# A hybrid decoder layer on one core: a reordered preparation, a fused second norm and an output projection cut into pieces

## The reference: what is computed

```
h     = rms_norm(x, norm1_g) * (1 + scale1) + shift1
x_lru, g_lru, q_lat, kv_lat, k_rope = split(h @ w_in)
lru   = rg_lru(causal_dwconv(x_lru)) * gelu(g_lru)          # recurrent half, 512 columns
attn  = latent attention(q_lat, kv_lat, k_rope, cache)      # attention half, 8 heads
mixed = concat(rms_norm(lru), rms_norm(attn)) @ w_o
x     = x + gate1 * mixed
h2    = rms_norm(x, norm2_g) * (1 + scale2) + shift2
up    = causal_dwconv(h2 @ w_up);  val, gt = split(up)
x     = x + gate2 * ((gelu(gt) * val) @ w_down)
```

## Time and profile before

| what | us |
|---|---|
| median of 3 runs | 986.07 |
| the runs | 986.3, 986.07, 982.07 |
| the profiled execution, its own time | 985.16 |
| its span, first to last instruction | 983.4 |
| busy in it: PE / DVE / ACT / POOL | 945.4 / 656.3 / 526.5 / 192.8 |

### The profile page before, as it was taken

One profiled execution on the slowest core, in us unless ns is written; L12 is line 12 of the kernel. 1 busy time (PEld: TensorE's weight loads), 2 busy tenths in 40 slices (PEclk: granted clock), 3 DMA queues, 4 the chain that ended last, 5 costly groups with the idle time before them and its releaser, 6 DMA issues.

```text
span 983.4 us, 20621 instructions
## 1 busy us (share of the span) xinstructions
PE 945.4 (96%) x7984; PEld 881.0 (90%) x7984; DVE 656.3 (67%) x1253; ACT 526.5 (54%) x1183; POOL 192.8 (20%) x192
## 2 busy tenths in 40 slices
PE   4799999899999999999999999999999999999997
PEld 2488876699999999999898989999999999999997
DVE  2695278478988988989873576777777777722221
ACT  2332854399889898898873333444444443312110
POOL 0022222133334333433340230010001001000000
PEclk9799999899999999999999989999999999999999
DMA  9968642400202202122121432333333332652202
GB/s 326 340 200 253 199 155 82 156 1 23 87 23 108 87 23 88 54 77 87 44 65 45 108 58 66 104 87 85 85 85 85 95 106 59 165 146 60 63 3 87
DMA packets 106289, 100.13 MB, mean 102 GB/s; under 512 B 7119, under 2 KB 94943, under 8 KB 104126
## 3 DMA queue, kind: packets, MB, share of 16 engines
q1 hardware_dynamic: 102422, 77.91, 27.2%
q0 software_dynamic: 3456, 20.97, 6.0%
q10 hardware_dynamic: 340, 0.27, 0.1%
HBM read 96.41 MB, written 2.94 MB: 101 GB/s over the span
## 4 chain that ended last, share of the span: by engine, by line
PE 88%; DVE 5%; ACT 3%; DMA 2%; issue 1%; SPq 0%; POOL 0%; DVEq 0%; ACTq 0%
PE ps L909 51%; PE ps L1297 19%; PE ps L904 7%; PE ps L942 2%; PE ps L1204 2%; PE ps L1255 2%; DMA RW<-w_ada 2%; PE ps L1292 1%; PE ps L1079 1%; PE ps L1230 1%; PE ps L915 1%; DVE normed_low L1904 1%; DVE RB L1878 0%; ACT RB L1493 0%; DVE RB L2334 0%
## 5 line engine op out<-in xcount | busy, mean ns | idle before, releaser
L909 PE MATMUL ps<-normed_high,up_weights_high 128*128 128x260 f32 x704 | 142.3, 283 | 0.2
L909 PE MATMUL ps<-normed_high,up_weights_low 128*128 128x260 f32 x704 | 142.0, 283 | 0.0
L909 PE MATMUL ps<-normed_low,up_weights_high 128*128 128x260 f32 x704 | 141.8, 283 | 0.0
L849 POOL TENSOR_TENSOR latents_low<-RB,latents_high 128x512 fp32r<-128x512 f32 (+1 forms) x72 | 86.2, 1197 | 163.9 <-ACT latents_high L1628 159.7
L1744 ACT ACTIVATE up_weights_high<-RW 128x1024 fp32r<-128x1024 f32 x44 | 46.5, 1060 | 133.5 <-PE ps L909 133.5
L1297 PE MATMUL ps<-key_weights_high,latents_high 128*128 128x260 f32 x528 | 116.4, 302 | 0.8 <-ACT RB L1675 0.7
L909 PEld LDWEIGHTS ps<-normed_high,up_weights_high 128*128 128x128 f32 x704 | 108.6, 189 | 0.8 <-DVE normed_low L1904 0.6
L909 PEld LDWEIGHTS ps<-normed_high,up_weights_low 128*128 128x128 f32 x704 | 108.6, 189 | 0.0
L909 PEld LDWEIGHTS ps<-normed_low,up_weights_high 128*128 128x128 f32 x704 | 108.3, 188 | 0.0
L1297 PE MATMUL ps<-key_weights_low,latents_high 128*128 128x260 f32 x528 | 106.4, 283 | 0.0
L1297 PE MATMUL ps<-key_weights_high,latents_low 128*128 128x260 f32 x528 | 106.4, 283 | 0.0
(11 more groups left out here) (331 smaller groups left out, 2197.1 us busy)
## 6 DMA issues: line engine op xcount, KB each, us to landing
RW<-w_ada SPq DMA_DIRECT2D x24, 1024.0 KB, 7.2
RW<-w_up SPq DMA_DIRECT2D x44, 512.0 KB, 5.0
RW<-w_down SPq DMA_DIRECT2D x8, 1408.0 KB, 7.2
RW<-w_in SPq DMA_DIRECT2D x11, 512.0 KB, 8.2
RB<-w_o SPq DMA_DIRECT2D x8, 512.0 KB, 4.1
RB<-x_prompt SPq DMA_DIRECT2D x2, 1024.0 KB, 13.3
o_y_p<-RB SPq DMA_DIRECT2D x4, 512.0 KB
cst<-consts SPq DMA_DIRECT2D x1, 845.0 KB, 11.6
```

The lines of the kernel that those rows point to most:

```text
L849: nc.gpsimd.tensor_tensor(latL[:, g % 3, c:4 * P], turned[:, g % 3, c:4 * P], latH[:, g % 3, c:4 * P].bitcast(F32), ALU.subtract).then_inc ...
L909: last = mm(ps[j % 4][rows[0]:rows[1], h, 0:H], lhsT, src[:, h * H:(h + 1) * H], start=start, stop=stop)
```

## The change

It edits three places.

**The preparation.** PE's order becomes: keys and values 0, the last modulation columns, keys and values 1, qst, keys and values 2, qa, keys and values 3, spread, three fillers, stored rows 0 to 3 with a filler behind each, the norm sum nlru, and only then the last stored rows. The copies of the stored rows go from VectorE to ScalarE. The squares of the recurrent half are added by GpSimd into one tile (three additions), and nlru is two matmuls in place of eight. GpSimd takes the samples' new rows later, inside unit 0. The slots of the jobs are dealt anew.

**The last softmax.** `recurrent_half` becomes `recurrent_part(m, ks)`, which runs only some of the four tiles. The eight fillers between the softmax's links give way to pieces of output tiles 1 and 2.

**The second norm.** VectorE makes x times gain times root in one instruction for all eight tiles; ScalarE adds the shift and writes the high part at once; VectorE makes the low part from the unrounded product, shift and high part. GpSimd's four products are gone. On PE the eight fillers ahead of the up-projection are gone, the first round of the loop is written out, and its first two jobs go through the tiles k as they become ready, the second job four tiles behind the first.

```diff
-PREP_ORDER = [("c5", 1), ("qst", 3), ("l0", 1), ("l1", 3), ("l2", 1), ("l3", 3), ("kv2", 2), ("kv3", 0), ("qa", 1), ("spread", 3),
-              ("l4", 1), ("l5", 3), ("l6", 2), ("nlru", 0)]
+PREP_ORDER = [("c5", 3), ("qst", 3), ("kv2", 1), ("qa", 3), ("kv3", 2), ("spread", 0), ("l0", 3), ("l1", 0), ("l2", 3), ("l3", 0),
+              ("nlru", 1), ("l4", 3), ("l5", 0), ("l6", 3)]
-J_NMLA, J_VP = job(2), job(3)
-J_WO = [job(n) for n in (0, 1, 7, 6, 4, 5, 11, 10)]
-J_N2, J_FST = job(KT), job(KT + 1)
+J_VP, J_NMLA = job(3), job(7)
+J_WO = [job(n) for n in (0, 1, 2, 11, 4, 5, 6, 8)]
+J_N2, J_FST = job(9), job(10)
...
@@ gpsimd @@
-            pool.wait_ge(s_clr, 4)
-            pool.wait_ge(s_new, 16)
+            for k in range(1, LT):
+                pool.wait_ge(s_sq, KT + 4 + k + 1)
+                if k > 1:
+                    pool.wait_ge(s_lrn, k - 1)
+                nc.gpsimd.tensor_tensor(lru_sq[:, 0, :], lru_sq[:, 0, :], lru_sq[:, k, :], ALU.add).then_inc(s_lrn, 1)
...
+                    if u == 0 and g == 1:
+                        pool.wait_ge(s_clr, 4)
+                        pool.wait_ge(s_new, 16)
+                        for n in range(2):
+                            new_key(n, n)
+                            new_latent(n, n)
...
-            pool.wait_ge(s_rs, 7)
-            for k in range(KT // 2, KT):
-                nc.gpsimd.tensor_tensor(h2[:, k, 0:NP], xT[:, k, 0:NP], rs[:, 0:NP], ALU.mult).then_inc(s_hq, 1)
@@ tensor @@
             keys_and_values(2)
-            keys_and_values(3)
...
+            keys_and_values(3)
             claim(pe, J_SPREAD)
...
+            keep_busy(spare, 3)
+            pe.wait_ge(s_kr, 2)
+            for a in range(4):
+                stored_rows(a)
+                keep_busy(spare, 1)
+            claim(pe, J_NLRU)
+            pe.wait_ge(s_lrn, LT - 1)
+            both(J_NLRU, ones, lru_sq[:, 0, :], True, True).then_inc(psum_full[J_NLRU % 4], 1)
             stored_rows(4)
...
-            for m in range(2):
-                pe.wait_ge(key_free[m], KEY_JOBS // 3)
-                recurrent_half(m)
-            pe.wait_ge(key_free[2], KEY_JOBS // 3)
+            recurrent_part(0, range(LT))
+            recurrent_part(1, (0,))
             turn_max(NS)
-            keep_busy(ps[2][:, 0, 0:2 * P], 2)
+            recurrent_part(1, (1,))
             spread_max(NS)
-            keep_busy(ps[2][:, 0, 0:2 * P], 4)
+            recurrent_part(1, (2, 3))
             pv(NS)
-            keep_busy(ps[2][:, 0, 0:2 * P], 2)
+            recurrent_part(2, (0,))
...
+            recurrent_part(2, (1,))
             pe.wait_ge(s_ol, 1)
...
-            recurrent_half(2)
+            recurrent_part(2, (2, 3))
             norm_sum(J_NMLA, LT, KT + 8)
-            recurrent_half(3)
+            recurrent_part(3, range(LT))
...
-            claim(pe, up_job(0), 0)
-            keep_busy(flat(up_job(0))[:, 0:2 * P], 8)
...
+            for k in range(KT):
+                pe.wait_ge(s_hlo, KT + k + 1)
+                up_products(0, 0, k)
+                if k >= KT // 2:
+                    up_products(0, 1, k - KT // 2)
+            for k in range(KT // 2, KT):
+                up_products(0, 1, k)
...
+            with pe.Fori(1, FT // 2) as i:
@@ scalar @@
+            def stored_rows(a):
...
+                A(otok[0:n, a, :], flat(j)[0:n, 0:KV + ROPE], ACT.Copy).then_inc(psum_free[j % 4], 1)
...
+            stored_rows(0)
             prep_rstd(8, HEADS)
+            for a in range(1, 4):
+                stored_rows(a)
             rstd(J_NLRU, LW).then_inc(s_rs, 1)
+            stored_rows(4)
+            stored_columns(0, 9)
+            stored_columns(1, 11)
...
-                A(h2[:, k, 0:NP], h2[:, k, 0:NP], ACT.Identity, bias=modT[:, 3 * KT + k, 0:1], scale=gmod[:, k, 0:1]).then_inc(s_h, 1)
+                act.wait_ge(s_hp, KT + k + 1)
+                A(hH[:, k, 0:NP], h2[:, k, 0:NP], ACT.Identity, bias=modT[:, 3 * KT + k, 0:1]).then_inc(s_h, 1)
@@ vector @@
+            def scaled(k):
+                V.scalar_tensor_tensor(h2[:, k, 0:NP], xT[:, k, 0:NP], gmod[:, k, 0:1], rs[:, 0:NP], MUL, MUL).then_inc(s_hp, 1)
+            def normed_low(k):
+                dve.wait_ge(s_h, KT + k + 1)
+                V.scalar_tensor_tensor(hL[:, k, 0:NP], h2[:, k, 0:NP], modT[:, 3 * KT + k, 0:1], hH[:, k, 0:NP].bitcast(F32), ADD, SUB).then_inc(s_hlo, 1)
...
+            for k in range(KT):
+                normed_low(k)
+                if k + 2 < KT:
+                    scaled(k + 2)
```

More of the change, by code:

```diff
@@ L836, in new_latent @@
                 nc.gpsimd.tensor_copy(lat[e][0:1, PAGES, :], newrow[0:1, s, 0:KV]).then_inc(s_newc, 1)
-            for n in range(2):
-                new_key(n, n)
-                new_latent(n, n)
             def low_latents(u, g):
@@ L1158, in _ @@
             stored_columns(1, XX, NP, 11)
-            j = J_NLRU
-            claim(pe, j)
-            for k in range(LT):
-                pe.wait_ge(s_sq, KT + 4 + k + 1)
-                last = both(j, ones, lru_sq[:, k, :], k == 0, k == LT - 1)
-            last.then_inc(psum_full[j % 4], 1)
             def kclaim(j):
@@ L2132, in _ @@
             dve.sem_inc(s_qbd, 1)
[L2133 to L2137 removed]
+            key_sums(3)
+            prep_keys(2)
+            prep_keys(3)
             def lru_normed():
```

98 lines of the change are left out of this document (44 added, 54 removed).

## The result

The changed kernel ran in 970.0, 970.85, 968.38 and 969.0 us, median 969.5, where the kernel before, with one more run, has a median of 986.18. The ratio is 0.984, with a 95% interval from 0.9824 to 0.9857. The forecast was 972.5 us in a range from 967 to 980. The profiled execution took 970.0 us, with a span of 968.2.

The account below looks back on a forecast made before the run. TensorE's own work fills 88% of the span, so only shortening its queue or waits counts. Gains of 6.0 (preparation), 3.1 (last softmax) and 4.0 (second norm) sum to 13.1 us, giving 972.5 us, range 967 to 980.

Parts of the forecast that it names:

- A: Preparation: reordered queue and shorter norm sum bring the first key product earlier; gain 6.0 us, ends 3.3 lost, 7.2 gained.
- The upper end, 7.2: Preparation: link-by-link sum without a new slow spell, first key product at 189.3 instead of 196.51; 7.2 us gained.
- the discount of 1.2 us: Preparation: held back for a possible lower-clock spell over fillers and stored rows, taking 6.0 us instead of 7.2.
- The row that spoke against the change: Preparation: GpSimd's additions might each cost a VectorE instruction 1.1 us, keys 1 on the path; worst case gain 4.9.
- B: Last softmax: output-tile pieces replace fillers, maxima turned sooner; gain 3.1 us, stretch 19.8 instead of 22.9, ends 2.0 and 3.6.
- the pieces lie in waits of their own size: Last softmax: pieces of 0.72, 1.44, 0.72 and 0.72 us fit TensorE's waits, leaving 0.3 us over for all four.
- C: Second norm: VectorE's fused chain and paced up-projection jobs start the third job earlier; gain 4.0 us, ends 0.7 and 5.3.
- The level was taken to fall for 6.5 us: Second norm: lower clock level from 578 to 584.5 slows 28 of 96 products; gain 4.5 us instead of 5.3.
- Rival 1: Clock takes the fillers' place: gaps from paced products and the longer thin preparation lower it; 979.6 us, chance 0.14.
- Rival 2: Preparation bound elsewhere: ScalarE's chain to the root 4 us later, gain there only 2 us; 976.5 us, chance 0.08.
- Rival 3: Last softmax: pieces do nothing, late weights of output tile 2 hold up the samples' result; 975.6 us, chance 0.05.
- rival 4: Slower: lower clock level entered at the paced start holds on through the loop; 991 us, chance 0.02.

Follow-up runs that it names:

- before_filled: Kernel before the change, with three fillers in the wait ahead of its first stored row and three ahead of its fifth; 985.16 us, ratio 0.9999.
- undo_norm2: Changed kernel with the second norm's diff taken back: GpSimd's four products, VectorE's old tiles, eight fillers, plain loop; 975.76 us, ratio 0.9892.
- undo_softmax_clean: Changed kernel, all slots kept, with only TensorE's order in the last softmax taken back; 972.69 us, ratio 0.9874.
- no_fillers6: Changed kernel without the six fillers ahead of unit 0, the seven new ones kept; 968.34 us, ratio 0.9822.
- undo_softmax_slot: Changed kernel with the old last softmax and old slots, but state's transposes in slot 2 and last output tile in slot 1; 976.9 us, ratio 0.9922.
- undo_softmax: Changed kernel with the old last-softmax order and the old slots of output projection, second norm and state's transposes; 984.44 us, ratio 0.9974.
- no_pacing: Changed kernel with the fused second norm kept, but eight fillers and the plain loop back at the up-projection's start; 972.91 us.
- norm_sum8: Changed kernel with the preparation's norm sum as eight matmuls, without GpSimd's three additions; 973.12 us, ratio 0.9875.
- no_fillers7: Changed kernel without the seven new fillers of the preparation; 971.24 us, ratio interval 0.9834 to 0.9878.
- no_fillers13: Changed kernel without the seven new preparation fillers and without the six ahead of unit 0; 967.17 us, ratio 0.9829.

## Why the prediction was right, point by point

**A, the preparation: 6.0 forecast, 7.17 measured.** The upper end, 7.2, was the right sum, link by link: the norm sum through at 181.6 (181.85 measured), VectorE's norm at 183.0 (183.29), the first low part at 187.1 (187.46), the cached rows' transposes at 184.0 (183.97), the first key product at 189.3 (189.27). The step that failed is the discount of 1.2 us for a new spell at the lower level, which did not come. Nor did the text see what before_filled shows: over half of the difference was two spells that the kernel before had. It counted them as given and so had the right sum for the pair of traces, without knowing what it was made of.

The row that spoke against the change, 1.78 us for a VectorE product beside GpSimd, did not carry over: keys 1 took 0.69 us at 173.53, inside GpSimd's additions from 173.51. In undo_norm2 the product of two SBUF tiles is back beside GpSimd and takes 1.78 again:

```profile
565.88 1.78 DVE L2343 TENSOR_TENSOR RB<-xT,rs 128x512 f32<-128x512 f32 x1 [3.05 <-ACT rs L1468]
```

The Trainium skill (GPSIMD Engine Reference, section 1. Specifications) puts the contention down to the SBUF interfaces that the two engines share, when VectorE reads two SBUF inputs. Both rows agree with it.

**B, the last softmax: 3.1 forecast, 2.79 measured** (20.14 us where 19.8 was forecast). The new waits are 0.79 and 0.15, against 0.9 and 0.3. The step that failed is that the pieces lie in waits of their own size. That holds at every link but one: from the samples' `OLR` products to their `OL` products it is 2.60 us where it was 2.17, since a piece of 0.72 us stands in a wait of 0.32. Before, and then after:

```profile
521.54 1.85 PE L1369 MATMUL ps<-cst,OLR 128*128 128x8 f32 x16
523.71 0.64 PE L1373 MATMUL ps<-OL,RB 128*64 128x8 f32 x16 [0.32 <-DVE OL L2289]
```

```profile
513.19 1.85 PE L1370 MATMUL ps<-cst,OLR 128*128 128x8 f32 x16
515.79 0.64 PE L1375 MATMUL ps<-OL,RB 128*64 128x8 f32 x16
```

The gain that I put down to order alone is in part one of slots, 0.37 us.

**C, the second norm: 4.0 forecast, 5.46 measured.** VectorE's chain was right: its last low part comes 576.88 - 564.82 = 12.1 us behind its first instruction, forecast 12.2, and the upper end of 5.3 was close. The third job stands 17.3 us behind that instruction, forecast 18.7. Two terms were mis-sized. The level was taken to fall for 6.5 us at a price of 0.8; in the changed kernel's trace it did not fall. That is luck, for it falls at this place in eight of the nine other traces with the paced start. In six of them, undo_softmax_clean and no_fillers6 among them, it cost nothing (403.32 to 403.41 us to the end, against 403.38): a small fall fits into TensorE's waits for VectorE, 0.34 us ahead of each of three tiles in the changed kernel. The price was right for a longer one: in undo_softmax_slot, with a granted clock of 0.79 and 0.53 there, the last stretch is 0.80 us longer. And the entry of the loop was put at 0.5 us; the chain shows no gap.

By the two traces the sum is 15.2 us where 13.1 was forecast. A and C, the two parts above their forecast, both held back something for a spell that did not come in the changed kernel's trace.

**What was not in the sum.** The units gave back 0.3 us. All four traces with the old preparation have 312.7 to 312.9 us for them, the ten with the new one 313.0 to 313.3. Unit 0 is not longer, the sign that GpSimd's later copies would have given: in the two first traces its key products agree to 0.02 us, and 0.15 us come in early in unit 1 and 0.20 early in unit 3. Which of the preparation's moves does that was not tried. And the prediction passed over the slots, though C depends on one: with the state's transposes left in slot 1, TensorE would have stood still for 9.0 us.

**The rivals.** Rival 1 (the clock takes the fillers' place) did not come: the granted clock is 1.00 in every window of the three places. It is not refuted for good, since the two kernels with the seven fillers left out show spells in the preparation, and most other traces one at the paced start. Rival 2 is out: TensorE doesn't wait for the root in the preparation, only 0.84 us for a copy. Rival 3 is out by undo_softmax_clean, rival 4 by the chain of the loop.

## What to carry to other kernels

When a wait is moved to an earlier place, follow every buffer that is claimed there to the instruction that frees it, and see what stands ahead of that on its engine; the wait that a profile prints may name another. Price a slow clock only where the engine is the one that is waited for: under the old fillers it cost 0.2 us at most, at the paced start nothing until it used up TensorE's waits and then 0.8 us, under the norm sum its whole length. Where executions differ in their early stages by more than an edit is worth, compare the stretches between fixed instructions before comparing totals.

## What the runs showed of the hardware that was not expected

The granted clock falls in some executions and not in others behind the same instructions. Eight traces with the new order and its seven fillers (after, undo_softmax, undo_norm2, no_pacing, undo_softmax_slot, undo_softmax_clean, no_fillers6, norm_sum8) were at 1.00 from 164 to 197 us; no_fillers7 fell to 0.50 at a place up to which its TensorE ran the same, and no_fillers13 only some 5 us behind that place. With the old order three traces of four fell. The Trainium skill (TensorE: Matmul & The Clock Gate, Part 1) has the lower level as the default, which sustained activity releases. The rows agree that falls come behind waits, as the 2.14 us in undo_softmax_slot, but waits of about 0.6 and 0.3 us stand ahead of that place in the traces that stayed up and in the one that fell, so TensorE's instructions and waits alone don't tell when. How often it falls in executions without a trace stays open: the mean granted clock of before_filled's ten executions, 0.983 to 0.990, is that of the kernel before (0.980 to 0.990), though its one trace was full in the preparation.
